# Mixture-of-experts phase: the low halves of the down weights are subtracted on GpSimd, and the ring slots are released by two semaphores

## Chip, cores and metric

One core of one Trainium2 chip runs the whole program in one launch. The metric is device time in microseconds (us), from start to end of the launch on that core.

## What is computed

The program is a two-layer hybrid backbone on 1024 tokens of width 1024. The change is in the last large part, the mixture of experts of layer 1 (top 2 of 8 experts, inner width 3584):

```python
def moe_ffn(h, w_router, w_g, w_u, w_d):
    b, t, d = h.shape
    hf = h.reshape(-1, d)
    logits = (hf @ w_router).astype(F32)
    top_v, top_i = lax.top_k(logits, TOP_K)
    gates = jax.nn.softmax(top_v, axis=-1)
    flat_e = top_i.reshape(-1)
    order = jnp.argsort(flat_e)
    tok = order // TOP_K
    xs = hf[tok]
    sizes = jnp.bincount(flat_e, length=N_EXPERTS).astype(jnp.int32)
    g = lax.ragged_dot(xs, w_g, sizes)
    u = lax.ragged_dot(xs, w_u, sizes)
    y = lax.ragged_dot(jax.nn.silu(g) * u, w_d, sizes)
    y = y * gates.reshape(-1)[order][:, None].astype(y.dtype)
    return jnp.zeros_like(hf).at[tok].add(y).reshape(b, t, d)
```

Everything is float32. In the kernel each float32 factor is split into a high half of type fp32r and a low half, the difference of the number and its high half, and a product is three matmuls: high by high, high by low, low by high.

## The kernel before

`phase_experts` works on 15 units of up to 256 rows (`NUNIT`), each with one expert. It is one loop (`Fori`) over units on each engine, with semaphores between the engines and a fixed order on each. The register `second` says whether a unit has a second tile of 128 rows; of a unit without one, called a one-tile unit here, TensorE does the first tile alone, while all other engines do the same work in each unit. The program's number b is the unit and q = 0 to 13 (`NP` = 14) is the slab of 256 inner columns.

The weights of a unit come in 42 chunks (`NCH`) of 128 x 2048 numbers, 1 MB each: for each q two chunks of the gate and up weights and one of the down weights. SyncE loads them in a fixed order into a ring of six slots, `wst` (L1650), in the order of `gu_chunk` and `dn_chunk`. A load waits until the chunk that was in its slot has been used up; before the change one semaphore, `split`, counts the used chunks of both kinds.

A chunk is used by two engines. ScalarE casts it to its high half (`gate_up_hi`, L1774; `down_hi`, L1780). VectorE then subtracts the high half from the chunk and writes the low half (`gate_up_lo`, L1838; `down_lo`, L1844), and adds one to `split`. Each of the high and low halves has two buffers, for even and odd q.

In step q TensorE does `gate_up(q)` (L1703, 24 matmuls of 512 columns for a tile), then `turn_product(q - 1)` (transposes, L1711), then `down(q - 2)` (L1723, 12 matmuls for a tile). ScalarE casts the chunks of q + 1, takes the silu of q (L1786), casts the turned product of q - 1 (L1791), and casts the down chunk of q - 1. VectorE subtracts the chunks of q + 1, multiplies silu and up of q (L1850), takes the low half of the product of q - 1 (L1855) and subtracts the down chunk of q - 1. These go on in program order on each engine.

The 15th step of a unit is its end. TensorE turns the rows of the next unit (L1684) in four parts and does `down(12)` and `down(13)` between them:

```python
pe.wait_ge(rl, b * 16 + 32)
turn_rows(0)
turn_product(NP - 1, tiles)
turn_rows(1)
pe.wait_ge(alr, b * NP + (NP + 1))
turn_rows(2)
down(NP - 2, tiles)
pe.wait_ge(xlr, b * 4 + 5)
turn_rows(3)
down(NP - 1, tiles)
```

ScalarE and VectorE split each part into `xh` (L1759) and `xl` (L1827). Part 3 is turned after `down(12)`, and on ScalarE its cast stands in front of the four casts of the next unit's chunks of q = 0 and 1. `gate_up(0)` of the next unit waits for the first two of the subtractions behind these.

GpSimd does no arithmetic in this phase. In each unit it issues the load of the rows after next (L1665, when the rows have been turned) and the store of the previous unit's result `y` (L1667, when it has been read out of PSUM), waits for that store to land and lets `y` be written again (`yfree`).

Of the kernel before, what the change touches and what calls it, by code (L numbers as in the profile page):

```python
# [14 lines left out]
F32 = mybir.dt.float32  # L15
# [4 lines left out]
ALU = mybir.AluOpType  # L20
# [1574 lines left out]
def phase_experts(nc, io, S, R):  # L1595
# [3 lines left out]
    NCH = 3 * NP  # L1599
    RING = 6  # L1600
    with Phase(nc, "moe") as ph:
# [14 lines left out]
        hi, split, gud, dnd = (ph.sem(n) for n in ("chunk_hi", "chunk_split", "gate_up_done", "down_done"))  # L1616
# [16 lines left out]

        def slot(n):

            return n % RING
# [3 lines left out]
        with nc.Block() as block:  # L1640

            @block.sync
            def _(sp):
                with sp.Fori(0, NUNIT) as b:
                    e = sp.value_load(R["expert"][0:1, bass.ds(b, 1)], min_val=0, max_val=NE - 1)

                    def load(n, p, part):
                        sp.wait_ge(split, b * NCH + (n + 1))
                        w = packed[bass.ds(e, 1), p, :, part * 2048:(part + 1) * 2048].rearrange("a p n -> p (a n)")
                        sp.dma_start(wst[:, slot(n), :], w).then_inc(wl[slot(n)], 16)  # L1650
# [9 lines left out]
            def _(pool):  # L1660
                pool.sem_inc(yfree, 1)
                pool.dma_start(rows[:, :, :], xs_b[1].rearrange("i p d -> p i d")).then_inc(rl, 16)
                with pool.Fori(0, NUNIT) as b:
                    pool.wait_ge(xtr, b * 4 + 4)
                    pool.dma_start(rows[:, :, :], xs_b[bass.ds(b + 2, 1)].rearrange("a i p d -> p (a i) d")).then_inc(rl, 16)  # L1665
                    pool.wait_ge(yev, b * 2 + 2)
                    pool.dma_start(ys_b[bass.ds(b, 1)].rearrange("a i p d -> p (a i) d"), y[:, :, :]).then_inc(yst, 16)  # L1667
                    pool.wait_ge(yst, b * 16 + 16)
                    pool.sem_inc(yfree, 1)
# [6 lines left out]
            def _(pe):  # L1676
# [15 lines left out]
                with pe.Fori(0, NUNIT) as b:  # L1692
                    second = pe.value_load(R["second"][0:1, bass.ds(b, 1)], min_val=0, max_val=1)

                    def gate_up(q, tiles):
                        pe.wait_ge(split, b * NCH + (RING + gu_chunk(q, 1) + 1))
# [17 lines left out]
                    def down(q, tiles):  # L1714
                        pe.wait_ge(alr, b * NP + (q + 3))
                        pe.wait_ge(split, b * NCH + (RING + dn_chunk(q) + 1))
# [101 lines left out]
            def _(dve):  # L1818
                dve.sem_inc(prod, 1)
                dve.sem_inc(alr, 2)  # L1820
                dve.sem_inc(split, RING)
# [9 lines left out]
                with dve.Fori(0, NUNIT) as b:  # L1831

                    def gate_up_lo(q):
                        for j in range(2):
# [4 lines left out]
                                                    guh[:, q % 2, k, :].bitcast(F32), ALU.subtract).then_inc(split, 1)  # L1839

                    def down_lo(q):
                        n = dn_chunk(q)
                        dve.wait_ge(hi, b * NCH + (n + 1))
                        nc.vector.tensor_tensor(dnl[:, q % 2, :, :], wst[:, slot(n), :].rearrange("p (k n) -> p k n", k=2),  # L1844
                                                dnh[:, q % 2, :, :].bitcast(F32), ALU.subtract).then_inc(split, 1)
# [17 lines left out]
                    for q in range(NP):  # L1863
# [7 lines left out]
                        if q >= 1:  # L1871
                            down_lo(q - 1)
# [3 lines left out]
                    down_lo(NP - 1)  # L1876
# [184 lines left out]
```

## Time and profile before

| | |
|---|---|
| median of 3 runs | 6741.96 us (6740.77 to 6745.71) |
| profiled execution, its own time | 6740.3 us |
| its span, first to last instruction | 6738.7 us |
| PE busy, share of the span | 5686.0 us, 84% |
| DVE busy | 2805.1 us, 42% |
| ACT busy | 1949.7 us, 29% |
| POOL busy | 263.7 us, 4% |
| mean granted TensorE clock | 0.915 of full speed |

PE is TensorE, PEld its weight loads, DVE VectorE, ACT ScalarE, POOL GpSimd, SP SyncE. Busy time of an engine says how long its instructions ran, not that it set the end. The experts' phase goes from about 3700 us to 6650 us of the span. A granted clock of 1.00 is 2.4 GHz, 0.5 is 1.2 GHz. In a row, "[3.71 <-DVE moe_down_lo L1844]" means that the engine stood idle for 3.71 us before the instruction, until that instruction of VectorE had ended.

### The profile page before, as it was taken

What the parts mean: (1) busy time and instruction counts of PE and PEld (TensorE: products, weight loads), DVE (VectorE), ACT (ScalarE), POOL (GpSimd) and SP (SyncE); (2) the same over time, 40 slices, a digit from 0 to 9 for tenths busy, and PEclk for the clock granted to TensorE, in tenths of its full rate; (3) what the DMA queues carried; (4) which work ended last, traced back from release to release, by engine and by line L of the source; (5) the groups of instructions that cost most, each with busy time, mean ns of one, the idle gap of its engine ahead of it and who ended that gap; (6) DMA issues with size and microseconds to landing.
All of it is one profiled execution on the core that took longest, in us unless ns stands there. A gap on an engine that the chain in (4) does not pass through costs nothing. (4 is left out here: it accounts for less than half of the span.)

```text
span 6738.7 us, 64137 instructions
## 1 busy us (share of the span) xinstructions
PE 5686.0 (84%) x24544; PEld 4418.1 (66%) x24545; DVE 2805.1 (42%) x2881; ACT 1949.7 (29%) x1904; POOL 263.7 (4%) x305
## 2 busy tenths in 40 slices
PE   8959955687998896991965899999999999999994
PEld 8945423466887773440644787787777778877773
DVE  0020037532111332006732744447568544466586
ACT  0000011121111321001110634336457433455473
POOL 0020001100000002000202000000000000000000
PEclk9979977798999998995975999999999999999996
DMA  6331010132111442110035955557569554566595
GB/s 199 112 112 33 13 63 1 57 117 66 61 61 59 169 140 79 39 56 2 1 113 193 351 200 182 181 200 288 213 246 352 209 190 167 213 240 254 194 352 210
DMA packets 314557, 1008.67 MB, mean 150 GB/s; under 512 B 58816, under 2 KB 141312, under 8 KB 231040
## 3 DMA queue, kind: packets, MB, share of 16 engines
q1 hardware_dynamic: 284240, 928.53, 38.2%
q0 software_dynamic: 13312, 50.34, 2.0%
q10 hardware_dynamic: 16688, 24.91, 1.0%
q8 instruction: 281, 4.60, 0.3%
q14 instruction: 36, 0.29, 0.0%
HBM read 912.73 MB, written 90.97 MB: 149 GB/s over the span
## 5 line engine op out<-in xcount | busy, mean ns | idle before, releaser
L1703 PE MATMUL ps<-moe_gate_up_hi,moe_xh 128*128 128x512 f32 x2576 | 1015.9, 394 | 81.2 <-DVE moe_gate_up_lo L1838 81.2
L1703 PE MATMUL ps<-moe_gate_up_hi,moe_xl 128*128 128x512 f32 x2576 | 1011.9, 393 | 0.0
L1703 PE MATMUL ps<-moe_gate_up_lo,moe_xh 128*128 128x512 f32 x2576 | 1011.2, 393 | 0.0
L1838 DVE TENSOR_TENSOR moe_gate_up_lo<-moe_wst,moe_gate_up_hi 128x2048 fp32r<-128x2048 f32 x420 | 941.4, 2286 | 54.5 <-ACT moe_gate_up_hi L1774 54.5
L1774 ACT CAST moe_gate_up_hi<-moe_wst 128x2048 fp32r<-128x2048 f32 x420 | 781.3, 1920 | 0.2
L1703 PEld LDWEIGHTS ps<-moe_gate_up_hi,moe_xh 128*128 128x128 f32 x2576 | 489.5, 190 | 190.6 <-DVE moe_gate_up_lo L1838 89.2
L1703 PEld LDWEIGHTS ps<-moe_gate_up_hi,moe_xl 128*128 128x128 f32 x2576 | 489.0, 190 | 103.3
L1703 PEld LDWEIGHTS ps<-moe_gate_up_lo,moe_xh 128*128 128x128 f32 x2576 | 489.6, 190 | 101.5
L1844 DVE TENSOR_TENSOR moe_down_lo<-moe_wst,moe_down_hi 128x2048 fp32r<-128x2048 f32 x210 | 481.3, 2292 | 148.0 <-ACT moe_down_hi L1780 147.6
L1850 DVE TENSOR_TENSOR moe_a<-moe_sil,ps 128x512 f32<-128x512 f32 x210 | 144.0, 686 | 892.6 <-ACT moe_sil L1786 892.6
L1786 ACT ACTIVATE moe_sil<-ps 128x512 f32<-128x512 f32 x210 | 125.9, 600 | 1329.6 <-PE ps L1703 1329.6
L1723 PE MATMUL ps<-moe_down_hi,moe_ah 128*128 128x512 f32 x1288 | 426.7, 413 | 53.9 <-DVE moe_down_lo L1844 53.9
L1299 PE MATMUL ps<-hh,up_wh 128*128 128x512 f32 (+1 forms) x1056 | 377.2, 357 | 51.9 <-DVE up_wl L1343 40.1
L1723 PE MATMUL ps<-moe_down_lo,moe_ah 128*128 128x512 f32 x1288 | 408.0, 399 | 0.0
L1723 PE MATMUL ps<-moe_down_hi,moe_al 128*128 128x512 f32 x1288 | 406.4, 397 | 0.0
L1780 ACT CAST moe_down_hi<-moe_wst 128x2048 fp32r<-128x2048 f32 x210 | 404.0, 1924 | 0.0
L433 PE MATMUL ps<-proj_w,hT 128*128 128x512 f32 x928 | 398.6, 592 | 0.0
L1299 PE MATMUL ps<-hl,up_wh 128*128 128x512 f32 (+1 forms) x1056 | 374.8, 355 | 0.0
L1299 PE MATMUL ps<-hh,up_wl 128*128 128x512 f32 (+1 forms) x1056 | 374.6, 355 | 0.0
L210 PE MATMUL ps<-ada_act,ada_w 128*128 128x2 f32 x1536 | 331.4, 353 | 35.5 <-DMA ada_w<-in_w_ada 27.4
L430 PE MATMUL ps<-hT,proj_w 128*128 128x512 f32 (+1 forms) x832 | 307.5, 533 | 59.9 <-DMA proj_w<-in_w_in 59.9
L210 PEld LDWEIGHTS ps<-ada_act,ada_w 128*128 128x128 f32 x1536 | 329.5, 332 | 37.1 <-issue 34.5
(317 smaller groups left out, 6874.0 us busy)
## 6 DMA issues: line engine op xcount, KB each, us to landing
moe_wst<-in_moe_packed SPq DMA_DIRECT2D x630, 1024.0 KB, 6.7
ada_w<-in_w_ada SPq DMA_DIRECT2D x24, 2048.0 KB, 8.4
down_wst<-in_ffn_w_down SPq DMA_DIRECT2D x66, 512.0 KB, 3.3
xs_d<-route_zero SPq DMA_DIRECT2D x1, 17408.0 KB, 54.3
proj_w<-in_w_in SPq DMA_DIRECT2D x8, 2048.0 KB, 7.9
four_dft<-in_dft_seq SPq DMA_DIRECT2D x16, 1024.0 KB, 4.9
moe_rows<-xs_d POOLq DMA_DIRECT2D x16, 1024.0 KB, 6.7
ys_d<-moe_y POOLq DMA_DIRECT2D x16, 1024.0 KB, 8.7
```

The lines of the kernel that those rows point to most:

```text
L210: mm = nc.tensor.matmul(ps[:, s % 2, 2 * m:2 * m + 2], wring[:, s, k, m * P:(m + 1) * P], act[:, k, :], start=(k == 0), stop=(k == KD - 1))
L430: mm = nc.tensor.matmul(ps[:, u % NB, :n], wring[:, i % 2, k, j * P:(j + 1) * P], hT[:, k, a:a + n], start=(k == 0), stop=(k == KD - 1))
L433: mm = nc.tensor.matmul(ps[:, u % NB, :], hT[:, k, a * P:(a + 1) * P], wring[:, i % 2, k, :], start=(k == 0), stop=(k == KD - 1))
L1299: x = nc.tensor.matmul(ps[:, 2 * g + kind, :n], w[:, s, kind, k, :], h[:, k, t0:t0 + n], start=(k == 0 and j == 0), stop=(k == KD - 1 and ...
L1703: x = nc.tensor.matmul(ps[:, 2 * (q % 2) + i, :], xx[:, k, t], w[:, q % 2, k, :], start=(k == 0 and j == 0), stop=(k == KD - 1 and j == 2))
L1723: x = nc.tensor.matmul(ps[:, Y0 + 2 * i + half, :], aa[:, q % 2, i, c, :], w[:, q % 2, c, half * 512:(half + 1) * 512], start=(q == 0 and ...
L1774: nc.scalar.copy(guh[:, q % 2, 4 * j:4 * j + 4, :], wst[:, slot(n), :].rearrange("p (k n) -> p k n", k=4)).then_inc(hi, 1)
L1780: nc.scalar.copy(dnh[:, q % 2, :, :], wst[:, slot(n), :].rearrange("p (k n) -> p k n", k=2)).then_inc(hi, 1)
L1786: nc.scalar.activation(sil[:, :, :], ps[:, 2 * (q % 2):2 * (q % 2) + 2, 0:W], ACT.Silu).then_inc(silu, 1)
L1838: nc.vector.tensor_tensor(gul[:, q % 2, k, :], wst[:, slot(n), :].rearrange("p (k n) -> p k n", k=4), guh[:, q % 2, k, :].bitcast(F32), AL ...
L1844: nc.vector.tensor_tensor(dnl[:, q % 2, :, :], wst[:, slot(n), :].rearrange("p (k n) -> p k n", k=2), dnh[:, q % 2, :, :].bitcast(F32), AL ...
L1850: nc.vector.tensor_tensor(a[:, q % 2, :, :, :].rearrange("p i c f -> p i (c f)"), sil[:, :, :], ps[:, 2 * (q % 2):2 * (q % 2) + 2, W:2 * W ...
```

## The change

The subtraction `down_lo` goes from VectorE's stream into GpSimd's. The operands, the buffers and the operation are the same. GpSimd does `down_lo(0)` between the issue of the rows' load and the issue of the store of `y`, and the 13 others after the store; its wait for the store's landing stands behind `down_lo(6)`. The semaphore `split` becomes two: `gsplit`, that VectorE raises, and `dsplit`, that GpSimd raises. A table (`PIECE`) says for each chunk which of the two a load has to wait for, and TensorE waits for `gsplit` before `gate_up` and for `dsplit` before `down`.

```diff
-        hi, split, gud, dnd = (ph.sem(n) for n in ("chunk_hi", "chunk_split", "gate_up_done", "down_done"))
+        hi, gsplit, dsplit, gud, dnd = (ph.sem(n) for n in ("chunk_hi", "gate_up_split", "down_split", "gate_up_done", "down_done"))
...
+        PIECE = {dn_chunk(q): (1, q) for q in range(NP)}
+        PIECE.update({gu_chunk(q, j): (0, 2 * q + j) for q in range(NP) for j in range(2)})
...
                     def load(n, p, part):
-                        sp.wait_ge(split, b * NCH + (n + 1))
+                        which, i = PIECE[(n - RING) % NCH]
+                        if which == 0:
+                            sp.wait_ge(gsplit, b * (2 * NP) + (i + 1 + (2 * NP if n >= RING else 0)))
+                        else:
+                            sp.wait_ge(dsplit, b * NP + (i + 1 + (NP if n >= RING else 0)))
...
+                pool.sem_inc(dsplit, NP)
                 with pool.Fori(0, NUNIT) as b:
+
+                    def down_lo(q):
+                        n = dn_chunk(q)
+                        pool.wait_ge(hi, b * NCH + (n + 1))
+                        nc.gpsimd.tensor_tensor(dnl[:, q % 2, :, :], wst[:, slot(n), :].rearrange("p (k n) -> p k n", k=2),
+                                                dnh[:, q % 2, :, :].bitcast(F32), ALU.subtract).then_inc(dsplit, 1)
+
                     pool.wait_ge(xtr, b * 4 + 4)
                     pool.dma_start(rows[:, :, :], xs_b[bass.ds(b + 2, 1)].rearrange("a i p d -> p (a i) d")).then_inc(rl, 16)
+                    down_lo(0)
                     pool.wait_ge(yev, b * 2 + 2)
                     pool.dma_start(ys_b[bass.ds(b, 1)].rearrange("a i p d -> p (a i) d"), y[:, :, :]).then_inc(yst, 16)
-                    pool.wait_ge(yst, b * 16 + 16)
-                    pool.sem_inc(yfree, 1)
+                    for q in range(1, NP):
+                        down_lo(q)
+                        if q == 6:
+                            pool.wait_ge(yst, b * 16 + 16)
+                            pool.sem_inc(yfree, 1)
...
-                        pe.wait_ge(split, b * NCH + (RING + gu_chunk(q, 1) + 1))
+                        pe.wait_ge(gsplit, b * (2 * NP) + (2 * NP + 2 * q + 2))
...
-                        pe.wait_ge(split, b * NCH + (RING + dn_chunk(q) + 1))
+                        pe.wait_ge(dsplit, b * NP + (NP + q + 1))
...
-                dve.sem_inc(split, RING)
+                dve.sem_inc(gsplit, 2 * NP)
...
-                    def down_lo(q):
-                        n = dn_chunk(q)
-                        dve.wait_ge(hi, b * NCH + (n + 1))
-                        nc.vector.tensor_tensor(dnl[:, q % 2, :, :], wst[:, slot(n), :].rearrange("p (k n) -> p k n", k=2),
-                                                dnh[:, q % 2, :, :].bitcast(F32), ALU.subtract).then_inc(split, 1)
...
-                        if q >= 1:
-                            down_lo(q - 1)
                     product_lo(NP - 1)
                     rows_lo(b * 4 + 4, 1)
                     rows_lo(b * 4 + 4, 2)
-                    down_lo(NP - 1)
                     rows_lo(b * 4 + 4, 3)
```

The end of a unit on VectorE, in its order before: the last product of a step (`moe_a`), the low halves of products (`moe_al`), of the down chunks 12 and 13 (`moe_down_lo`) and of the next rows (`moe_xl`).

```order
L1850 TENSOR_TENSOR moe_a<-moe_sil,ps 128x512
L1855 TENSOR_TENSOR moe_al<-ps,moe_ah 128x512
L1825 ISA
L1827 TENSOR_TENSOR moe_xl<-ps,moe_xh 128x4x128
L1843 REGISTER_ALU
L1844 TENSOR_TENSOR moe_down_lo<-moe_wst,moe_down_hi 128x2048
L1855 TENSOR_TENSOR moe_al<-ps,moe_ah 128x512
L1825 REGISTER_ALU
L1827 TENSOR_TENSOR moe_xl<-ps,moe_xh 128x4x128
```

With the change the same place reads as follows; the down chunk is gone from it and nothing else moved.

```order
L1863 TENSOR_TENSOR moe_a<-moe_sil,ps 128x512
L1868 TENSOR_TENSOR moe_al<-ps,moe_ah 128x512
L1844 ISA
L1846 TENSOR_TENSOR moe_xl<-ps,moe_xh 128x4x128
L1868 TENSOR_TENSOR moe_al<-ps,moe_ah 128x512
```

GpSimd's stream at the start of the loop over units, after the change: the first subtraction stands between the two DMA issues, and behind the store come the 13 others, alternating with register operations.

```order
+L1680 ISA
+L1680 DMA moe_rows<-xs_d 128x2x1024
+L1675 ISA
+L1676 TENSOR_TENSOR moe_down_lo<-moe_wst,moe_down_hi 128x2048
+L1682 ISA
+L1683 ISA
+L1683 DMA ys_d<-moe_y 128x2x1024
+L1675 REGISTER_ALU
+L1676 TENSOR_TENSOR moe_down_lo<-moe_wst,moe_down_hi 128x2048
```

The store of `y` now stands one subtraction later in GpSimd's stream; the rows' load stands where it was.

## Rows read from the trace of the kernel before

**Rows 1.** Waits between 3700 and 6650 us: who waited for whom, total, times, longest.
```profile
PE ps L1703 <- DVE moe_gate_up_lo L1838: 81.2, 22, 8.4
...
PE ps L1723 <- DVE moe_down_lo L1844: 53.9, 15, 3.7
```

**Rows 2.** Stretches: length, busy and count by engine, clock, DMA share, GB/s.
```profile
3758.40:3766.90 8.50, 8.50 (x40) 7.01 (x39) 7.97 (x6) 6.49 (x5) 0.00 (x0) 1.00 0.98 398
...
3950.00:4000.00 50.00, 50.00 (x228) 41.38 (x227) 23.58 (x16) 19.14 (x15) 0.00 (x0) 1.00 0.51 188
```

**Rows 3.** Timeline of the first one-tile unit, PE, two steps apart: start, us, engine, line, operation.
```profile
3744.90 0.39 PE L1703 MATMUL ps<-moe_gate_up_hi,moe_xh 128*128 128x512 f32 x1
...
3761.75 0.39 PE L1703 MATMUL ps<-moe_gate_up_hi,moe_xh 128*128 128x512 f32 x1
```

**Rows 4.** The same unit, VectorE and ScalarE.
```profile
3737.71 2.29 DVE L1844 TENSOR_TENSOR moe_down_lo<-moe_wst,moe_down_hi 128x2048 fp32r<-128x2048 f32 x1 [0.23 <-ACT moe_down_hi L1780]
3739.92 4.49 DVE L1838 TENSOR_TENSOR moe_gate_up_lo<-moe_wst,moe_gate_up_hi 128x2048 fp32r<-128x2048 f32 x2
...
3751.51 1.92 ACT L1780 CAST moe_down_hi<-moe_wst 128x2048 fp32r<-128x2048 f32 x1
```

**Rows 5.** Timeline of GpSimd: the rows' loads, 15 in all, first and last among them.
```profile
3714.09 0.73 POOL L1665 DMA_DIRECT2D moe_rows<-xs_d  x1 [11.52 <-PE ps L1684]
...
5107.08 0.70 POOL L1665 DMA_DIRECT2D moe_rows<-xs_d  x1 [120.41 <-PE ps L1684]
...
5242.44 0.70 POOL L1665 DMA_DIRECT2D moe_rows<-xs_d  x1 [120.75 <-PE ps L1684]
...
5488.56 0.70 POOL L1665 DMA_DIRECT2D moe_rows<-xs_d  x1 [231.51 <-PE ps L1684]
...
5736.63 0.70 POOL L1665 DMA_DIRECT2D moe_rows<-xs_d  x1 [233.46 <-PE ps L1684]
...
5985.59 0.70 POOL L1665 DMA_DIRECT2D moe_rows<-xs_d  x1 [234.34 <-PE ps L1684]
...
6503.19 0.70 POOL L1665 DMA_DIRECT2D moe_rows<-xs_d  x1 [120.56 <-PE ps L1684]
```

**Rows 6.** Timeline of the end of a one-tile unit.
```profile
3840.67 2.29 DVE L1844 TENSOR_TENSOR moe_down_lo<-moe_wst,moe_down_hi 128x2048 fp32r<-128x2048 f32 x1 [1.11 <-ACT moe_down_hi L1780]
...
3843.01 1.22 PE L1723 MATMUL ps<-moe_down_hi,moe_ah 128*128 128x512 f32 x2 [3.71 <-DVE moe_down_lo L1844]
...
3848.75 0.71 PE L1723 MATMUL ps<-moe_down_hi,moe_ah 128*128 128x512 f32 x2
...
3849.03 0.59 ACT L1759 CAST moe_xh<-ps 128x512 fp32r<-128x512 f32 x1 [5.13 <-PE ps L1684]
...
3857.41 0.80 PE L1703 MATMUL ps<-moe_gate_up_hi,moe_xh 128*128 128x512 f32 x1 [5.65 <-DVE moe_gate_up_lo L1838]
```

**Rows 7.** GpSimd's groups by line: count, busy, mean ns.
```profile
L1070 POOL TENSOR_TENSOR FM<-FM,TM 128x2560 f32<-128x2560 f32 x1 | 5.6, 5587 | 30.9 <-ACT TM L1062 30.9
L1070 POOL TENSOR_TENSOR FM<-FM,TM 128x2048 f32<-128x2048 f32 x1 | 4.5, 4505 | 30.0 <-ACT TM L1062 30.0
```

**Rows 8.** VectorE and GpSimd side by side in an earlier phase, then GpSimd by itself.
```profile
3595.14 1.17 DVE L344 SCALAR_TENSOR_TENSOR hF<-xF,gmod,nf_rstd 128x512 f32<-128x512 f32 x1
3594.87 1.78 POOL L354 TENSOR_SCALAR hF<-hF,mod 128x512 f32<-128x512 f32 x1
...
3600.14 1.56 POOL L354 TENSOR_SCALAR hF<-hF,mod 128x512 f32<-128x512 f32 x1
...
L344 DVE SCALAR_TENSOR_TENSOR hF<-xF,gmod,nf_rstd x16: 739/751/1179, 3581.4 to 3598.7; 128x512 f32<-128x512 f32 x16
```

**Rows 9.** Two lines that run side by side in the scan: ns, minimum, median, maximum.
```profile
L968 POOL TENSOR_TENSOR scan_qg<-qd,cst x40: 1038/1043/1044, 1096.9 to 3360.5; 128x512 f32<-128x512 f32 x40
...
L997 DVE TENSOR_TENSOR scan_ex<-scan_ex,ps x40: 662/670/680, 1105.9 to 3378.5; 128x512 f32<-128x512 f32 x40
```

**Rows 10.** DMA between 3750 and 3834 us: issues of the weight chunks.
```profile
moe_wst<-in_moe_packed SPq DMA_DIRECT2D x30, 1024.0 KB, 7.3
```

More of the change, by code:

```diff
@@ L1838, in gate_up_lo @@
                             nc.vector.tensor_tensor(gul[:, q % 2, k, :], wst[:, slot(n), :].rearrange("p (k n) -> p k n", k=4),
-                                                    guh[:, q % 2, k, :].bitcast(F32), ALU.subtract).then_inc(split, 1)
-                    def down_lo(q):
-                        n = dn_chunk(q)
-                        dve.wait_ge(hi, b * NCH + (n + 1))
-                        nc.vector.tensor_tensor(dnl[:, q % 2, :, :], wst[:, slot(n), :].rearrange("p (k n) -> p k n", k=2),
-                                                dnh[:, q % 2, :, :].bitcast(F32), ALU.subtract).then_inc(split, 1)
+                                                    guh[:, q % 2, k, :].bitcast(F32), ALU.subtract).then_inc(gsplit, 1)
                     def product(q):
```

## The prediction

> **What bounds the kernel now.** I read the waits of the experts' phase first, then the busy time of short stretches, then the timelines of one step and of one end of a unit.
>
> The waits [rows 1] show how rarely TensorE stands still: 22 times for the low halves of gate and up (81.2 us) and 15 times, once in each unit, for `down_lo` (53.9 us, so 3.6 us each). The second is the wait that this change touches.
>
> The stretches [rows 2] show two kinds of unit. With two tiles TensorE is busy for 50.00 of 50 us and VectorE for 23.58. In a one-tile unit TensorE is busy for 8.50 of 8.50 us, but VectorE for 7.97 and the DMA engines for 0.98 of the time: three things are nearly full at once. Two steps there last 3761.75 - 3744.90 = 16.85 us, so one lasts 8.43 [rows 3]. So TensorE sets a step, and VectorE has about half a microsecond to spare in a one-tile step.
>
> The rows' loads [rows 5] cut the phase into units, since each is issued when the rows have been turned. From 5107.08 to 5242.44 a one-tile unit lasts 135.4 us, from 5242.44 to 5488.56 a two-tile unit 246.1, and from 5736.63 to 5985.59 one lasts 249.0. From the first to the last load there are 14 units, 6 with one tile and 8 with two; the last, with one tile, follows.
>
> **What the change does, part by part.**
>
> *VectorE's relief.* 210 subtractions of 2.29 us go from its stream. I cost this at nothing. In two-tile units VectorE is half idle. In one-tile steps TensorE has no idle time [rows 2, 3], so nothing there waits for a low half. At the starts of units TensorE waits for the casts and subtractions of gate and up [rows 6], among which no `down_lo` stands.
>
> *The length of the subtraction on GpSimd.* The trace has one of just this shape, two inputs in SBUF and 2048 numbers in a partition: 4505 ns [rows 7]. The 2560-number one is 1082 ns longer, 2.1 ns a number, so it is work and not overhead. I take 4.50 us against 2.29, which is 2.21 us more. The output here is fp32r, which no row of GpSimd shows; on VectorE it makes no difference that a row would show.
>
> *Ends of units.* There the wait is exposed. The cast of down chunk 12 ends, the subtraction runs from 3840.67, and TensorE starts `down(12)` at 3843.01 after 3.71 us of idling [rows 6]. Behind `down(12)` come the turning of part 3 (its cast starts at 3849.03), the casts for the next unit, and `gate_up(0)` of the next unit at 3857.41. All this moves by what the subtraction gets longer: 15 x 2.21 = **33.2 us**. Chunk 13 adds nothing: GpSimd would have done it at 3840.67 + 2 x 4.50 = 3849.67, and TensorE gets to `down(13)` at 3848.75 + 2.21 = 3850.96.
>
> *Clock behind a longer pause.* In the one-tile end above, a matmul pair that follows the 3.71 us pause takes 1.22 us, against 0.71 for the same pair at 3848.75 [rows 6]: half clock. Two-tile ends have nearly the same pause and only some are slowed, which I read from the lengths of their units, 246.1, 248.1 and 249.0 us [rows 5]. The mean of all eight is (6503.19 - 3714.09 - 6 x 135.4) / 8 = 247.1. A pause of 3.6 + 2.2 = 5.8 us should put all of them at the slow end: 8 x (249.0 - 247.1) = **15 us**. From below this is nothing; from above I allow twice that.
>
> *One-tile steps: two engines at the same memory.* The subtraction on GpSimd and both subtractions of gate and up on VectorE read two inputs from SBUF. An earlier phase shows such a meeting [rows 8]: VectorE's operation with two SBUF inputs takes 1.17 us beside a GpSimd operation and mostly 0.74 to 0.75, and GpSimd's takes 1.78 beside 1.56. So they hold each other up. Where VectorE has one input in PSUM, as in `moe_a` and `moe_al`, they don't: 40 GpSimd operations lie within 1038 to 1044 ns beside VectorE operations within 662 to 680 [rows 9].
>
> How much do they hold each other up here? From below: VectorE lost 1.17 - 0.74 = 0.43 us to a GpSimd operation with one input of 512; with two inputs of 2048 that is 8 x 0.43 = 3.44 us. From above: the whole GpSimd instruction, 4.50 us. The SBUF page of the Trainium skill (SBUF — State Buffer, section on the two separate sides) calls it an exclusive lock for the whole instruction, against which the other "fully blocks". The row disagrees for its case, since 0.43 us is much less than the instruction's 1.56. By that page the sum is 6842 us, by the row 6795.
>
> I take the upper bound: GpSimd's two-input time grows by 2.1 ns a number, while two readings at the rate of that row would be 2 x 0.43 / 512 = 1.7 ns, so reading lasts most of the instruction in any case, and if it is paced by the work, all of it.
>
> Then a one-tile step has 4.50 us of GpSimd and 4.49 us of VectorE [rows 4] that exclude each other: 8.99 us against 8.43. VectorE's pair can start when GpSimd is done, and `gate_up` behind the pair. The first meeting is in the step at 3737.71 [rows 4]: GpSimd to 3742.21, the pair to 3746.70, where `gate_up(3)` now starts at 3744.90 [rows 3], 1.80 us late. Ten more pairs follow in the unit, each 0.56 us behind: 1.80 + 5.6 = 7.4 us, in 7 units **52 us**. With a hold of 3.44 us the first meeting costs 3741.15 + 4.49 - 3744.90 = 0.74 us and a step has 7.93 us of it, under 8.43: 5 us in all. A step gets longer from a hold of 8.43 - 4.49 = 3.94 us on. In two-tile steps 8.99 us lie beside nearly twice the time, at no cost.
>
> *Ring.* A slot with a down chunk becomes free 2.2 us later. Now that of chunk 0 is free at 3737.71 + 2.29 = 3740.00, a load lands 7.3 us after its issue [rows 10], at 3747.3, and ScalarE casts from that slot next, for q = 2, at 3751.51 [rows 4]. Of 4.2 us there remain 2.0, and more if the steps get longer. No cost, as long as other chunks keep the queue full.
>
> *GpSimd's DMA issues.* The rows' load stands in front of `down_lo(0)` as before. The store of `y` waits for `down_lo(0)` now, some 14 us in a one-tile unit, and `y` is written again only a unit later, over 130 us away. SyncE's waits are as many as before, on two counters.
>
> **Sum.** 33 + 15 + 52 = 100 us on the profiled execution's own 6740.3 us is 6840.3. The median of the runs shown is 1.7 us higher, so I say **6842 us**.
>
> **Rivals.**
>
> *Short hold (0.24).* GpSimd holds VectorE up only while it reads, 3.44 us. Rows 8 speak for it; the doubt is whether a two-input operation reads ahead like that. Cost: 33 + 15 + 5 = 53, or 6795 us.
>
> *Only the longer subtraction (0.09).* No hold worth a row and clock as it is now: 33 us, 6775. It needs the pause to leave the clock alone, against the half clock in rows 6.
>
> *The ring runs dry (0.06).* DMA is at 0.98 of a one-tile stretch [rows 2], which moves at 398 GB/s there; 3.15 MB need 7.9 us of each 8.43. A slot that opens 2.2 us later with nothing else queued would leave at most 2.2 - 0.5 = 1.7 us of idle DMA in each of about 77 steps, 130 us more, beside 33 from the ends: 6905. Against it: 7.3 us to land with 2.6 us of a chunk's transfer means that two or more are always queued.
>
> *Faster (0.05).* GpSimd does the subtraction as fast as VectorE, so that `down(12)` waits 3.6 us as now, and the moved instructions shift the half clock away from the ends of the 7 one-tile units. The 5.7 us between `down(12)` and `down(13)` there would be about 3.1 at full clock: 7 x 2.6 = 18 us less, 6724. It decides only if the subtraction takes under about 2.3 us; at 4.50 [rows 7] the 15 ends lose more than that.
>
> *No change that can be told (0.06).* Some 13 us, 0.2%, is about what a measurement of this kernel can tell from nothing. It needs a subtraction under 3.2 us at every end and no hold.
>
> The forecast has 0.50. It would be 6827 with no clock loss and 6865 if the handovers between the engines add 0.3 us in each of 77 steps. The range of 6772 to 6868 takes that in with the first two rivals, and leaves out the ring, the faster case and no change. Chances: faster 0.05, same 0.06, slower 0.89.
>
> **What the profile after would show.** `down_lo` on GpSimd at about 4.5 us where VectorE is idle; TensorE's 15 waits for it at 5.8 us each, near 87 us in all; units of two tiles at about 249 + 2 us; subtractions of gate and up on VectorE that take up to 6.7 us instead of 2.29 in one-tile units, and steps of 9.0 us there with a pause of 0.5 us before `gate_up`. If VectorE's mean stays near 2.3 us, the hold is wrong; if GpSimd's time at the ends of units isn't 4.5, the first term is; if ScalarE waits for chunks, the ring is the cause.

## The result, and the profile after

| | before | after |
|---|---|---|
| median | 6741.36 us, 4 runs (6736.05 to 6745.71) | 6828.31 us, 4 runs (6827.52 to 6829.70) |
| profiled execution, its span | 6738.7 us | 6828.1 us |
| DVE busy | 2805.1 us | 2794.7 us |
| POOL busy | 263.7 us | 1243.7 us |
| mean granted TensorE clock | 0.915 | 0.912 |

The changed kernel is slower: the ratio is 1.013, with a 95% interval of 1.0112 to 1.0147, some 87 us. The forecast was 6842 us. VectorE issues 210 subtractions fewer and yet is busy for as long as before. That is the first sign of a hold.

The page of the profile after, its line of busy times and the two groups of subtractions (columns: count, busy us, mean ns, idle time before them):

```profile
PE 5718.1 (84%) x24544; PEld 4417.6 (65%) x24545; DVE 2794.7 (41%) x2671; ACT 1949.0 (29%) x1904; POOL 1243.7 (18%) x515
...
L1857 DVE TENSOR_TENSOR moe_gate_up_lo<-moe_wst,moe_gate_up_hi 128x2048 fp32r<-128x2048 f32 x420 | 1396.6, 3367 | 345.5 <-ACT moe_gate_up_hi L1793 345.5
L1676 POOL TENSOR_TENSOR moe_down_lo<-moe_wst,moe_down_hi 128x2048 fp32r<-128x2048 f32 x210 | 979.9, 4670 | 1963.1 <-ACT moe_down_hi L1799 1963.1
```

A pair of subtractions of gate and up took 4.49 us before [rows 4]; the mean of one is now 3367 ns. The 210 of the down chunks took 2.29 us each on VectorE and take 4.67 on GpSimd.

The waits of the experts' phase after, as in [rows 1] (total us, times, longest):

```profile
PE ps L1742 <- POOL moe_down_lo L1676: 89.5, 22, 6.0
PE ps L1722 <- DVE moe_gate_up_lo L1857: 89.4, 66, 8.4
```

The wait for `down_lo` has gone from 53.9 to 89.5 us. Seven of the 22 are short, 1.6 us in all, as a variant below lists apart; the 15 at the ends have 87.9. The wait for gate and up has gone from 22 times to 66 times. In the trace 46 of them are new: seven of 1.3 us, one at the first meeting of GpSimd and VectorE in each one-tile unit, and 39 of some 0.2 us, 16.6 us in all. Two long ones at ends of two-tile units are missing from this line, since their releaser now reads "issue" (3.90 and 3.95 us). The idle time of PE doesn't show all that the steps lost, so I read the steps by their length.

**One step of a one-tile unit.** VectorE and GpSimd, timelines after (start, length), and then the busy times of a stretch of one step's length, to be laid beside [rows 2]:

```profile
3740.70 4.62 POOL L1676 TENSOR_TENSOR moe_down_lo<-moe_wst,moe_down_hi 128x2048 fp32r<-128x2048 f32 x1 [23.12 <-ACT moe_down_hi L1799]
3742.45 5.01 DVE L1857 TENSOR_TENSOR moe_gate_up_lo<-moe_wst,moe_gate_up_hi 128x2048 fp32r<-128x2048 f32 x1 [2.04 <-ACT moe_gate_up_hi L1793]
...
3758.50 4.64 POOL L1676 TENSOR_TENSOR moe_down_lo<-moe_wst,moe_down_hi 128x2048 fp32r<-128x2048 f32 x1 [4.35 <-ACT moe_down_hi L1799]
3760.26 7.23 DVE L1857 TENSOR_TENSOR moe_gate_up_lo<-moe_wst,moe_gate_up_hi 128x2048 fp32r<-128x2048 f32 x2 [0.56 <-ACT moe_gate_up_hi L1793]
3767.34 4.64 POOL L1676 TENSOR_TENSOR moe_down_lo<-moe_wst,moe_down_hi 128x2048 fp32r<-128x2048 f32 x1 [4.20 <-ACT moe_down_hi L1799]
```

```profile
3758.40:3767.30 8.90, 8.81 (x39) 6.85 (x38) 8.34 (x5) 6.55 (x7) 4.64 (x1) 1.00 1.00 412
```

At the first meeting GpSimd is at work until 3740.70 + 4.62 = 3745.32. VectorE's subtraction begins at 3742.45 and ends at 3747.46, which is GpSimd's end and 2.14 us more. It takes 2.28 us alone, so it lost 2.73 of the 2.87 us that were left of GpSimd's instruction, all but the last 0.14. Later GpSimd ends at 3763.14 and VectorE's pair at 3767.49, 4.35 us behind it, and the next of GpSimd starts at 3767.34. The two engines take turns: 4.64 + 4.35 - 0.15 = 8.84 us, and the next step has 8.96. Before, a step lasted 8.43 us [rows 3]. What released GpSimd in these rows is ScalarE's cast, though, and that is taken up with the variant that moves the cast.

From silu to silu the 13 intervals of a one-tile unit sum to 112.2 us against 105.5. The first meeting is in a step of 10.47 instead of 8.43, and ten more have a mean of 8.90: 2.04 + 4.7 = 6.7 us a unit, 47 us in 7 units. The steps of two-tile units are what they were, 16.80 us.

**One end of a unit.** Timeline of PE and GpSimd at the end of the same unit as [rows 6]:

```profile
3850.39 9.04 POOL L1676 TENSOR_TENSOR moe_down_lo<-moe_wst,moe_down_hi 128x2048 fp32r<-128x2048 f32 x2 [7.26 <-ACT moe_down_hi L1799]
3854.96 1.22 PE L1742 MATMUL ps<-moe_down_hi,moe_ah 128*128 128x512 f32 x2 [5.98 <-POOL moe_down_lo L1676]
...
3868.46 0.79 PE L1722 MATMUL ps<-moe_gate_up_hi,moe_xh 128*128 128x512 f32 x1 [5.67 <-DVE moe_gate_up_lo L1857]
```

TensorE idles for 5.98 us instead of 3.71 before `down(12)`. The idle time before `gate_up(0)` is 5.67 and was 5.65, so nothing of the delay is won back.

Three of GpSimd's loads of rows after, to be laid beside [rows 5]:

```profile
3860.73 0.72 POOL L1680 DMA_DIRECT2D moe_rows<-xs_d  x1 [1.31 <-PE ps L1703]
4111.46 0.72 POOL L1680 DMA_DIRECT2D moe_rows<-xs_d  x1 [5.13 <-PE ps L1703]
...
4361.71 0.72 POOL L1680 DMA_DIRECT2D moe_rows<-xs_d  x1 [4.18 <-PE ps L1703]
```

A two-tile unit now lasts 4111.46 - 3860.73 = 250.7 or 4361.71 - 4111.46 = 250.3 us. All eight have a mean of 250.2, against 247.2. The one-tile units last 143.9 to 144.7, against 135.0 to 135.6. Eight times 3.0 and seven times 9.0 is 87 us: the whole difference lies in the units.

### The profile page after: what moved, and what is told of

Read it like the earlier page. It is cut to its first block and busy times, and to the rows that moved or that the text cites. A ratio compares the mean times of both kernels' runs of the same rounds, so it can differ in the third digit from the quotient of the medians.

```text
span 6828.1 us, 64139 instructions
## 1 busy us (share of the span) xinstructions
PE 5718.1 (84%) x24544; PEld 4417.6 (65%) x24545; DVE 2794.7 (41%) x2671; ACT 1949.0 (29%) x1904; POOL 1243.7 (18%) x515
## 5 line engine op out<-in xcount | busy, mean ns | idle before, releaser
L1857 DVE TENSOR_TENSOR moe_gate_up_lo<-moe_wst,moe_gate_up_hi 128x2048 fp32r<-128x2048 f32 x420 | 1396.6, 3367 | 345.5 <-ACT moe_gate_up_hi L1793 345.5
L1676 POOL TENSOR_TENSOR moe_down_lo<-moe_wst,moe_down_hi 128x2048 fp32r<-128x2048 f32 x210 | 979.9, 4670 | 1963.1 <-ACT moe_down_hi L1799 1963.1
L1722 PE MATMUL ps<-moe_gate_up_hi,moe_xh 128*128 128x512 f32 x2576 | 1025.4, 398 | 100.8 <-DVE moe_gate_up_lo L1857 89.4
L1722 PEld LDWEIGHTS ps<-moe_gate_up_hi,moe_xh 128*128 128x128 f32 x2576 | 489.0, 190 | 240.8 <-DVE moe_gate_up_lo L1857 136.8
L1742 PE MATMUL ps<-moe_down_hi,moe_ah 128*128 128x512 f32 x1288 | 431.4, 417 | 89.5 <-POOL moe_down_lo L1676 89.5
L354 POOL TENSOR_SCALAR hT<-hT,mod 128x512 f32<-128x512 f32 (+1 forms) x48 | 70.2, 1480 | 1729.0 <-DVE hT L344 1729.0
```

The source lines that it names most:

```text
L1676: nc.gpsimd.tensor_tensor(dnl[:, q % 2, :, :], wst[:, slot(n), :].rearrange("p (k n) -> p k n", k=2), dnh[:, q % 2, :, :].bitcast(F32), AL ...
L1722: x = nc.tensor.matmul(ps[:, 2 * (q % 2) + i, :], xx[:, k, t], w[:, q % 2, k, :], start=(k == 0 and j == 0), stop=(k == KD - 1 and j == 2))
L1742: x = nc.tensor.matmul(ps[:, Y0 + 2 * i + half, :], aa[:, q % 2, i, c, :], w[:, q % 2, c, half * 512:(half + 1) * 512], start=(q == 0 and ...
L1857: nc.vector.tensor_tensor(gul[:, q % 2, k, :], wst[:, slot(n), :].rearrange("p (k n) -> p k n", k=4), guh[:, q % 2, k, :].bitcast(F32), AL ...
```

## The experiments

Each is told by its difference from the kernel before, which ran beside it on the same chip. My theory had two separate costs, one at the ends of units and one in the steps of one-tile units. The first three variants take the change apart.

**Two semaphores alone.** The subtraction goes back to VectorE, and the rest of the change stays.

```diff
-                    def down_lo(q):
-                        n = dn_chunk(q)
-                        pool.wait_ge(hi, b * NCH + (n + 1))
-                        nc.gpsimd.tensor_tensor(...)
...
+                    def down_lo(q):
+                        n = dn_chunk(q)
+                        dve.wait_ge(hi, b * NCH + (n + 1))
+                        nc.vector.tensor_tensor(...)
```

> The changed kernel, but the subtraction of the down chunks stays on VectorE at its old place; only the two semaphores are left of the change. Theory (the 87 us are GpSimd's: a longer subtraction at the ends of units, and VectorE held up by it in one-tile steps): the time of the kernel before, 6741 us within 10. Rival (the release by two semaphores delays the loads of the ring): some or all of the 87 us stay, with ScalarE waiting for chunks.

Measured: 6740.81 us (10 runs), ratio 0.9998 (0.9989 to 1.0008) to a kernel before of 6742.28. Its waits hold the line of [rows 1] unchanged:

```profile
PE ps L1732 <- DVE moe_down_lo L1853: 53.9, 15, 3.7
```

The second semaphore and the table of what a load waits for cost nothing and bring nothing. All of the 87 us is in the move.

**The ends on VectorE.** GpSimd keeps chunks 0 to 11, VectorE does 12 and 13 in the places of before.

```diff
-                    for q in range(1, NP):
+                    for q in range(1, NP - 2):
                         down_lo(q)
...
+                        if q == NP - 1:
+                            down_lo(q - 1)
...
+                    down_lo(NP - 1)
```

> The changed kernel, but the down chunks 12 and 13 of each unit are subtracted by VectorE again. Theory: the end term goes (15 waits of TensorE for the low half of chunk 12 back from 5.9 to 3.6 us, some half clock with them), the steps of one-tile units stay at 8.89 us: 6828 - 40 = 6788 us. Rival (it is all contention and the ends don't matter): under 10 us off 6828.

**Only the ends on GpSimd.** The reverse: 12 and 13 on GpSimd, 0 to 11 on VectorE. In both of these variants the engine waits in addition until the low half of the chunk before is done, so that the one counter stays in order.

```diff
-                    for q in range(1, NP):
-                        down_lo(q)
...
+                    down_lo(NP - 2)
+                    down_lo(NP - 1)
...
+                        if 1 <= q < NP - 1:
+                            down_lo(q - 1)
```

> The opposite: only the down chunks 12 and 13 of each unit are subtracted by GpSimd, the other twelve by VectorE. Theory: steps of one-tile units 8.43 us as before, ends as in the changed kernel: 6741 + 40 = 6781 us. If the two parts add up, this gain and that of the run before sum to 87 us within 10; if one hides the other they don't.

Measured: with the ends on VectorE 6785.21 us, ratio 1.0066 (1.0049 to 1.0083), 43 us over before. With only the ends on GpSimd 6780.14, ratio 1.0056 (1.0039 to 1.0073), 38 us over. Together 81 of the change's 87, equal within the intervals. The waits of TensorE for the down chunks, first with the ends on VectorE, then with them on GpSimd:

```profile
PE ps L1742 <- DVE moe_down_lo L1864: 53.9, 15, 3.7
...
PE ps L1742 <- POOL moe_down_lo L1676: 1.6, 7, 0.3
```

```profile
PE ps L1741 <- POOL moe_down_lo L1677: 88.0, 15, 6.0
```

In the first the ends are those of before, the two-tile units too (246.0 to 247.8 us), but the steps of one-tile units still have 8.90 us and those units last 141.7 to 142.4: 7 x 6.7 = 47 us. In the second the steps have 8.43 us, one-tile units are 2.3 us longer than before and two-tile units 3.0: 7 x 2.3 + 8 x 3.0 = 40 us. So the two costs are separate, and they add up.

**What holds VectorE.** The next two put another operation of GpSimd in the place of the subtraction. Eight of the 1024 columns of each half are still subtracted, so that the order of waits stays; beyond them both kernels leave out the low halves of the down weights. In the first the rest is filled with zeros, which only writes to SBUF; in the second it is copied from the chunk, which reads one input.

```diff
-                        nc.gpsimd.tensor_tensor(dnl[:, q % 2, :, :], ...)
+                        nc.gpsimd.tensor_tensor(dnl[:, q % 2, :, 0:8], ...)
...
+                        nc.gpsimd.memset(dnl[:, q % 2, :, 8:].bitcast(mybir.dt.bfloat16), 0.0).then_inc(dsplit, 1)
```

> The changed kernel, but instead of the subtraction GpSimd subtracts the first 8 columns of each half and fills the rest with zeros (as 2-byte numbers, to last some 3.4 us), so the low halves of the down weights are left out. It reads nearly nothing from SBUF. Theory (GpSimd's reads hold up VectorE's two-input instructions): every subtraction of gate and up takes 2.29 us, one-tile steps are 8.43 us, and only the ends are longer or shorter by the fill's length minus 2.29. Rival (any GpSimd instruction that long does it, or the lateness of the low half itself): steps stay over 8.6 us.

```diff
+                        nc.gpsimd.tensor_copy(dnl[:, q % 2, :, 8:], wst[...][:, :, 8:]).then_inc(dsplit, 1)
```

> The changed kernel, but GpSimd subtracts the first 8 columns of each half and copies the rest of the chunk (one input from SBUF), so the low halves of the down weights are left out. By the earlier phase's 0.43 us for 512 numbers of one input the hold would be 1.7 us from its start, which is over when VectorE starts its first subtraction 1.75 us later: VectorE at 2.29 us, one-tile steps of 8.43 us. If instead a GpSimd instruction holds VectorE to its end whatever it reads, the first subtraction of each pair takes 2.29 plus the rest of the copy.

Measured, one run each, beside a kernel before of 6738.71 us: the fill 6766.94, the copy 6745.61 (nine runs of before lay between 6736 and 6748, so the copy can't be told from it). The durations of the tiles with the fill (ns: minimum, median, maximum), then with the copy:

```profile
L1679 POOL MEMSET moe_down_lo<- x210: 3474/3484/3487, 3739.8 to 6659.2; 128x4064 bf16 x105
...
L1859 DVE TENSOR_TENSOR moe_gate_up_lo<-moe_wst,moe_gate_up_hi x420: 2280/2287/2295, 3719.0 to 6639.4; 128x2048 fp32r<-128x2048 f32 x140
```

```profile
L1679 POOL CAST moe_down_lo<-moe_wst x210: 1872/1885/1892, 3743.6 to 6637.9; 128x2032 fp32r<-128x2032 f32 x105
...
L1859 DVE TENSOR_TENSOR moe_gate_up_lo<-moe_wst,moe_gate_up_hi x420: 2276/2286/2467, 3722.9 to 6618.8; 128x2048 fp32r<-128x2048 f32 x140
```

With the fill of 3.48 us not one of VectorE's 420 subtractions is lengthened, though in the trace 165 of them start inside a fill that has 1.9 us to go. That an engine is busy at the same SBUF is no cost by itself. Its 28 us lie at the ends: 15 waits of 5.0 us, one-tile units of 136.8 and two-tile units of 249.0.

The copy does hold VectorE. Timeline with the copy, GpSimd and VectorE:

```profile
3767.71 1.89 POOL L1679 CAST moe_down_lo<-moe_wst 128x2032 fp32r<-128x2032 f32 x1
...
3769.31 2.43 DVE L1859 TENSOR_TENSOR moe_gate_up_lo<-moe_wst,moe_gate_up_hi 128x2048 fp32r<-128x2048 f32 x1 [2.59 <-ACT moe_gate_up_hi L1795]
```

The copy ends at 3769.60. VectorE starts 0.29 us earlier and loses 0.15, so it ends at 3771.74, 2.14 us after GpSimd, just as it did behind the subtraction: 2.14 to 2.15 us in each of the 165 places with the copy, 2.14 to 2.16 in the 165 of the changed kernel where GpSimd's subtraction comes first. One input or two, the hold lets go 0.14 us before GpSimd's end. It is small here only because the copy takes 1.89 us and is nearly through when VectorE comes. A hold only while GpSimd reads isn't ruled out for the copy: at the rate of [rows 8], 0.43 us for 512 numbers, its 2032 would hold for 1.71 us from its start, and it held for 1.89 - 0.15 = 1.74.

**Columns halved.** If the two engines take turns, a shorter turn should end the cost of the steps. GpSimd subtracts one half of each down chunk and VectorE the other.

```diff
-                        nc.gpsimd.tensor_tensor(dnl[:, q % 2, :, :], ...)
+                        nc.gpsimd.tensor_tensor(dnl[:, q % 2, 0, :], wst[:, slot(n), 0 * 1024:(0 + 1) * 1024], ...)
...
+                        nc.vector.tensor_tensor(dnl[:, q % 2, 1, :], wst[:, slot(n), 1 * 1024:(1 + 1) * 1024], ...)
```

> The changed kernel, but GpSimd subtracts the first 1024 columns of each down chunk and VectorE the other 1024, in the place where it did all of it. GpSimd should take 4.64 / 2 = 2.3 us, VectorE 1.2. Theory (both exclude each other in reading, and a step gets longer only when the sum passes 8.43 us): 2.3 + 1.2 + 4.35 = 7.9 us, so one-tile steps of 8.43 us; at the ends the halves still go one behind the other, 3.5 us instead of 2.29, so TensorE's 15 waits are 4.8 us each: 6741 + 18 = 6759 us. Rival (the hold is a delay for each meeting, whatever the lengths): steps over 8.6 us. Rival for the ends (halves run side by side): waits of 3.6 us, 6741.

Measured: 6767.22 us, ratio 1.0039 (1.0025 to 1.0053), 24 us over before. The durations of both halves:

```profile
L1866 DVE TENSOR_TENSOR moe_down_lo<-moe_wst,moe_down_hi x210: 1224/1227/3452, 3738.1 to 6658.3; 128x1024 fp32r<-128x1024 f32 x105
L1677 POOL TENSOR_TENSOR moe_down_lo<-moe_wst,moe_down_hi x210: 2395/3411/3460, 3738.2 to 6658.4; 128x1024 fp32r<-128x1024 f32 x105
```

The steps have 8.43 us again, as expected of turns that sum to less than that. The first step in which the engines meet has 9.3, which I hadn't expected, 6 us in 7 units. Most of the rest is the ends, where a wait has 4.75 us instead of 3.6, 17 us in 15 of them. The second row shows the hold in the other direction: GpSimd's half takes 2.4 us alone, and mostly 3.41 us, since VectorE's half of 1.23 us goes first.

**ScalarE's cast first.** Another reading of the 8.90 us was a chain: GpSimd waits for ScalarE's cast, which waits for the silu, which waits for TensorE, which waits for VectorE. The rows of the changed kernel allow it as well:

```profile
3750.79 7.71 DVE L1857 TENSOR_TENSOR moe_gate_up_lo<-moe_wst,moe_gate_up_hi 128x2048 fp32r<-128x2048 f32 x2
3758.55 0.50 PE L1722 MATMUL ps<-moe_gate_up_hi,moe_xh 128*128 128x512 f32 x1
3764.38 0.60 ACT L1805 ACTIVATE moe_sil<-ps 128x512 f32<-128x512 f32 x1 [2.35 <-PE ps L1722]
3765.34 1.92 ACT L1799 CAST moe_down_hi<-moe_wst 128x2048 fp32r<-128x2048 f32 x1
```

VectorE's pair ends at 3758.50, the cast at 3767.26, GpSimd starts at 3767.34, and the pair that it holds ends at 3769.10 + 7.23 = 3776.33: two steps in 17.83 us, 8.9 each. To take the chain away, ScalarE casts the down chunk ahead of the silu in all steps of a unit but the last.

```diff
+                        if q >= 1 and q < NP - 1:
+                            down_hi(q - 1)
                         silu_of(q)
...
                         if q == NP - 1:
                             rows_hi(b * 4 + 4, 0)
-                        if q >= 1:
                             down_hi(q - 1)
```

> The changed kernel, but in every step except the last of a unit ScalarE casts the down chunk right behind the casts of gate and up, before its silu. Two readings of the 8.89 us step: either the sum of GpSimd's and VectorE's times that exclude each other (4.64 + 4.35 less a little overlap) sets it, then steps stay within 8.8 to 9.0 us and the time within 10 us of 6828; or a chain over two steps does (gate_up 5.45, silu and casts 2.9, GpSimd 4.64, VectorE's pair 4.35, together 17.8), then taking silu and the product's cast out of it shortens two steps by 1.1 us or more, 77 steps by 0.4 us or more, 30 us or more off the time.

Measured: 6883.57 us, ratio 1.0214 (1.0196 to 1.0231), 145 us over before. Neither reading had this. The timeline of GpSimd, one row of VectorE from the same stretch, and one from the unit's first meeting:

```profile
3763.45 5.33 POOL L1676 TENSOR_TENSOR moe_down_lo<-moe_wst,moe_down_hi 128x2048 fp32r<-128x2048 f32 x1 [9.58 <-ACT moe_down_hi L1799]
3771.87 5.76 POOL L1676 TENSOR_TENSOR moe_down_lo<-moe_wst,moe_down_hi 128x2048 fp32r<-128x2048 f32 x1 [3.09 <-ACT moe_down_hi L1799]
3780.29 6.19 POOL L1676 TENSOR_TENSOR moe_down_lo<-moe_wst,moe_down_hi 128x2048 fp32r<-128x2048 f32 x1 [2.66 <-ACT moe_down_hi L1799]
3788.73 6.62 POOL L1676 TENSOR_TENSOR moe_down_lo<-moe_wst,moe_down_hi 128x2048 fp32r<-128x2048 f32 x1 [2.25 <-ACT moe_down_hi L1799]
3797.15 4.83 POOL L1676 TENSOR_TENSOR moe_down_lo<-moe_wst,moe_down_hi 128x2048 fp32r<-128x2048 f32 x1 [1.80 <-ACT moe_down_hi L1799]
...
3793.49 10.63 DVE L1858 TENSOR_TENSOR moe_gate_up_lo<-moe_wst,moe_gate_up_hi 128x2048 fp32r<-128x2048 f32 x2 [1.00 <-ACT moe_gate_up_hi L1793]
...
3738.07 11.36 DVE L1858 TENSOR_TENSOR moe_gate_up_lo<-moe_wst,moe_gate_up_hi 128x2048 fp32r<-128x2048 f32 x2 [0.69 <-ACT moe_gate_up_hi L1793]
```

GpSimd starts every 8.43 us, so the steps keep TensorE's pace for a while: with the cast early, what GpSimd does isn't on TensorE's path. But its instruction gets 0.43 us longer each time, and each starts with VectorE already at its pair. Its ends lie 8.85 to 8.87 us apart, the 4.50 + 4.35 us of two turns. By the fourth row it ends at 3795.35, after VectorE's next pair has begun at 3793.49. GpSimd's next subtraction gets in at 3797.15, between the two of that pair, and the pair takes 10.63 us instead of 4.49. The step has some 12.5 us, and it comes again in the unit. The first meeting, at 3738, is of the same kind: GpSimd gets in between the two of the pair, and the step has 14.8. These three are all of the 14.5 us that the unit's 13 intervals are longer than before. So turns that sum to more than a step can be put off, but when the debt falls due it is paid by the engine that TensorE waits for, and TensorE, busy in all of a one-tile step [rows 2], can't win a late step back. The run doesn't decide between the two readings of the changed kernel, since it brought in a new loss of its own. It shows that turns alone, with no chain in the way, need 8.85 us, so that a step can't stay under that; the chain would give nearly the same, 8.9, and it too has GpSimd's hold in it.

**The casts and subtractions of the end moved earlier.** Both costs at the end come from an order: down chunk 12 is cast behind the silu and the product of the last slab, and chunk 13 behind the next rows' parts. This variant starts from the kernel before. On ScalarE chunk 12 goes ahead of the last slab's silu, and chunk 13 behind the cast of the next rows' part 0, where chunk 12 was. The diff shows ScalarE; VectorE's `down_lo` is moved in the same way.

```diff
+                        if q == NP - 1:
+                            down_hi(NP - 2)
                         silu_of(q)
...
                         if q == NP - 1:
                             rows_hi(b * 4 + 4, 0)
-                        if q >= 1:
+                            down_hi(NP - 1)
+                        elif q >= 1:
                             down_hi(q - 1)
...
-                    down_hi(NP - 1)
```

> The kernel before, with one edit: in the last slab's step ScalarE casts down chunk 12 before its silu instead of after the cast of the next rows, and VectorE subtracts it before its product; chunk 13 follows the rows' part 0. Theory (what made the ends expensive is that the cast and the subtraction of chunk 12 start after TensorE needs them, and each length of theirs is paid in full): the pause of 3.6 us before down(12) goes in all 15 units, 6741 - 54 = 6687 us, and with less half clock down to 6665. Rival (another wait is right behind, for chunk 13 or for the next unit's rows): under 20 us faster.

The same early casts on ScalarE in the changed kernel, with the subtraction on GpSimd, whose order needs no edit:

> The changed kernel with ScalarE's cast of down chunk 12 before the silu of the last slab and that of chunk 13 behind the rows' part 0; GpSimd subtracts as soon as they are there. Theory (two separate costs): the end term goes with the pause, 5.9 us in 15 units, and the steps of one-tile units stay at 8.89 us: 6741 + 47 - 54 = 6734 us, down to 6710 with less half clock. Rival (VectorE's and GpSimd's exclusion also bites at the ends): over 6760.

Measured: on VectorE **6663.69 us**, ratio 0.9882 (0.9866 to 0.9899), 79 us under before; on GpSimd 6717.98, ratio 0.9966 (0.9954 to 0.9979), 21 us under the 6738.71 of the kernel before beside it. The first beats both kernels. TensorE's waits in it, and its wait for the down chunks with the subtraction on GpSimd:

```profile
PE ps L1703 <- DVE moe_gate_up_lo L1840: 74.6, 22, 8.4
...
PE ps L1723 <- DVE moe_al L1857: 8.5, 7, 1.2
```

```profile
PE ps L1742 <- POOL moe_down_lo L1676: 21.4, 14, 2.8
```

On VectorE the wait for `down_lo` is gone from the list, 53.9 us, and with it the half clock at that place: the pair of `down(12)` takes 0.72 us, not 1.22 [rows 6]. A one-tile unit lasts 129.3 to 129.9 us, on average 5.6 less, and a two-tile unit 242.2 to 242.7, 4.8 less: 7 x 5.6 + 8 x 4.8 = 78, of the 79. With GpSimd the wait for `down_lo` shrinks to 21.4 us, nearly all of it seven waits of 2.8 us at ends of one-tile units, while the steps of one-tile units stay at 8.90 us. The two differ by 58 us (79 less 21), of which the steps are 47. So even where every end is early, the subtraction on GpSimd costs more than it gives.

**Part 3 of the rows later.** In the variant above the next thing waited for is `gate_up(0)`, behind part 3 of the next rows. I moved that part's cast and subtraction behind those of the next unit's first two chunks. The diff shows ScalarE; VectorE's `rows_lo` is moved in the same way.

```diff
-                for s in range(4):
+                for s in range(3):
...
+                    rows_hi(b * 4, 3)
...
-                    rows_hi(b * 4 + 4, 3)
```

> The kernel with the early cast of down chunk 12 (all subtractions on VectorE), and one more edit of the same sort: part 3 of the next rows is cast and subtracted at the start of the next unit, behind the casts and subtractions of its first two chunks instead of ahead of them. Theory (at the ends TensorE pays for an order, not for the amount of work): the wait of gate_up(0) for the low half of its chunks, 5.65 us in the kernel before, shrinks to the part that isn't covered by down(13), 3 to 5 us less in 15 units, so 6664 - 60 = 6604 us within 20. Rival (another wait is right behind, for the ring's loads or for the rows' low half): under 20 us.

Measured: 6665.38 us, ratio 0.9887 (0.9871 to 0.9904). The gain that I expected over the variant above isn't there. PE at the start of the second unit, later part first, then the variant above:

```profile
3855.10 0.63 PE L1703 MATMUL ps<-moe_gate_up_hi,moe_xh 128*128 128x512 f32 x1 [4.79 <-issue]
```

```profile
3852.23 0.79 PE L1703 MATMUL ps<-moe_gate_up_hi,moe_xh 128*128 128x512 f32 x1 [4.74 <-DVE moe_gate_up_lo L1840]
```

The pause is as long, but its releaser now reads "issue": TensorE waited for nothing that another engine does. The sequencer's own rows for the line of the loop over units say what it was, later part first, then the variant above (ns: minimum, median, maximum):

```profile
L1692 PEldq COMPARE_BRANCH  x15: 83/6192/6597, 3847.4 to 6564.2; - x15
```

```profile
L1692 PEldq COMPARE_BRANCH  x15: 83/6117/6484, 3844.6 to 6561.7; - x15
```

Fourteen of the fifteen branches jump back to the start of the loop, and take some 6.1 us; the fifteenth, at 6564.2, leaves the loop and takes 0.083. With the part later the jump starts at 3847.44 and lasts 6.49 us, to 3853.93, with `gate_up(0)` 1.2 us behind it. The low half of the gate and up chunks was ready at 3853.43. So I had taken away one of two things of nearly the same length. To put the second away one would write the loop out on TensorE, or let the unit's last instructions stand behind the jump; neither was tried.

## Why the prediction was right, and where its sizes were off

- **Ends, 33.2 us.** Right. TensorE's 15 waits have a mean of 5.86 us instead of 3.6 (5.98 at one-tile ends, 5.76 at two-tile ends), 87.9 - 53.9 = 34 us. They came back alone in the variant with only the ends on GpSimd. The subtraction is 4.51 to 4.57 us there, as the 4505 ns of [rows 7] said.
- **Clock behind a longer pause, 15 us.** Right in sign and too large. Two-tile units are 3.0 us longer, of which 2.27 are the subtraction; 8 x 0.7 is some 6 us. The term was mis-sized: the forecast put all eight at the slow end, 249.0 us and the longer pause, and less the pause's growth they lie at 247.1 to 248.5, with a mean of 247.9. A longer pause lengthened the half clock (6.8 to 13.7 us of a two-tile unit, 3.4 to 10.2 before) without making the units alike. The mean of before that the forecast used was 247.1 and is 247.2, since it took one unit's 135.4 for all with one tile. The variants with waits of 4.75 to 5.0 us, the halves and the fill, have two-tile units of 248.5 to 249.2, those with 5.76 us have 249.3 to 250.8.
- **Steps of one-tile units, 52 us.** Right in mechanism, measured 47. The hold lasts until 0.14 us before the end of GpSimd's instruction, close to the upper of my two bounds, and the variant with the ends on VectorE shows its price by itself. The term was mis-sized twice: a turn of VectorE behind GpSimd is 4.35 us and not 4.49, and a turn of GpSimd is 4.64 and not 4.50, with a handover that overlaps by 0.15, so ten steps have 0.47 us each and not 0.56; the first meeting cost 2.04 us and not 1.80. The forecast had only the turns; a chain through ScalarE's cast, which it didn't have, fits the same rows, and no run sets the two apart in the changed kernel. Of the rule that I weighed, from the Trainium skill (SBUF — State Buffer, section on the two separate sides), this case's rows bear out the whole-instruction hold, but for the last 0.14 us, for a GpSimd operation with two inputs: 5.01 us for one of 2.28, and in the other direction 3.41 for one of 2.4. The row of the earlier phase [rows 8], taken as its rival, was not typical of an operation with two inputs: by its rate the hold would be 3.44 us, and it is 4.62 - 0.14 = 4.48.
- **VectorE's relief, nothing.** Right. Nothing waited for a `down_lo` in the steps, and what VectorE gave away, 210 x 2.29 = 481 us, it nearly got back as time in which it is held, 420 x 1.08 = 454 us (mean 3.367 us, and 2.286 before).
- **Ring and GpSimd's issues, nothing.** Right. ScalarE waits for no chunk in the list of waits after, and a chunk's load lands in 7.6 us between 3750 and 3834 us, 7.3 before [rows 10]. Two semaphores alone change nothing.
- **The sum.** 34 + 6 + 47 is 87 us, and so much do the medians differ. The span of the profiled execution grew by 89.4, of which 2.8 us lie before the first load of rows (3716.85 after, 3714.09 before), where nothing was changed. The 14 us between the forecast and the median are the clock term, 9, and the steps, 5.
- **The rivals.** A short hold, or only the longer subtraction, would have left steps of 8.43 us; they have 8.90. The ring never ran dry. Faster needed a subtraction under 2.3 us.

What stays open is what ends the hold. Behind the subtraction and behind the copy it lets go 0.14 us before GpSimd's end, but the copy's 1.74 us of hold are also what the rate of [rows 8] gives. In [rows 8] themselves VectorE's operation starts 0.27 us into GpSimd's and ends at 3596.31, 0.34 us before it, so there the hold doesn't last to the end. A hold while GpSimd reads fits all three if the subtraction reads for nearly all of its time; no run tested that, or measured an operation like that of the row, one with one input and an operand of one number a partition.

## What to carry to other kernels

Before moving an elementwise operation with two SBUF inputs from VectorE to GpSimd, add GpSimd's duration to that of VectorE's own two-input operations in the same step: the sum must be under the step, since they take turns, and here 4.50 + 4.35 = 8.85 against 8.43 us was too much. With half of each chunk the sum was under it, and the steps kept their 8.43 us. Price its length also at each place where TensorE waits for it, in full, however much room the steps have. Where a producer is late, look first for where its instruction stands in its own engine's order: to cast and subtract two chunks earlier brought 79 us, while the engine with more idle time cost 87.

## What the runs showed of the hardware that I had not expected

- The hold depends on whether GpSimd's operation reads. Beside a subtraction with two inputs of 2048 numbers and beside a copy with one of 2032, VectorE's two-input subtraction ends 2.14 to 2.16 us after GpSimd, where it takes 2.28 alone. Beside a fill of 3.48 us, which only writes, none of 420 is held.
- A copy with one input of 2032 numbers takes 1.89 us on GpSimd, a subtraction with two of 2048 takes 4.5. The one with the second input takes more than twice as long; whether the input or the operation makes the difference was not tested.
- TensorE's jump back to the start of the loop over units takes some 6.1 us, against 0.083 where it isn't taken. The Trainium skill (Runtime: NRT & Kernel Launch, section on instruction fetch mechanics) says that a taken branch to a target outside the fetched pages forces a fetch of it before execution can go on. The rows agree with that in kind, and the number is theirs; that it is this fetch and nothing else was not tested. In the kernel before it lies beside the pause at the start of a unit, and shows only when that pause is shortened.
- Two engines that exclude each other can drift against each other at 0.43 us a step, without any cost to be seen, until one slips in between two instructions of the other.
